# Hybrid decoder step, expert stage: bound-checked gather and scatter of taken slots, with expert outputs kept at a row of token and choice

## What is computed

```python
g_sel = argmax(t @ rc_w + rc_b)                  # one of 4 groups for each token
vals, idx = top_k(softmax(lf[g_sel]), 2)         # two of the 8 experts in it
eid = g_sel * 8 + idx                            # 32 experts in all
for e in range(32):
    h = silu(t @ w_gate[e]) * (t @ w_up[e])      # 1024 -> 512
    out = out + gates[:, e:e+1] * (h @ w_down[e])  # 512 -> 1024
```

## Time and profile before

| | |
|---|---|
| median of three runs | 1232.8 us |
| profiled execution, its own time | 1232.51 us |
| its span in the trace | 1230.7 us |
| TensorE busy | 1017.0 us (83%) |
| VectorE, ScalarE, GpSimd busy | 32%, 23%, 24% |
| bytes moved | 291.19 MB, mean 237 GB/s |

### The profile page before, as it was taken

How to read it: one execution, slowest core, us unless ns; L and a number is a source line. 1 busy time by engine, 2 the same in 40 slices (tenths; PEclk the granted TensorE clock), 3 DMA queues, 4 the chain that set the end, 5 groups by cost and what they waited for, 6 DMA issues and landing times.

```text
span 1230.7 us, 16173 instructions
## 1 busy us (share of the span) xinstructions
PE 1017.0 (83%) x6140; PEld 692.2 (56%) x6141; DVE 399.5 (32%) x678; ACT 281.5 (23%) x554; POOL 299.4 (24%) x480
## 2 busy tenths in 40 slices
PE   5999999896999974699964999999976778976760
PEld 3888789675674763577743555555533434543430
DVE  3998374532423328651233101011000001000006
ACT  3125224530222604341121121121201111111102
POOL 1000788884014593035002001010100000000003
PEclk8999999897997896899985999999999999999895
DMA  5685341110057550415464999999999999999976
GB/s 214 241 137 84 75 106 36 37 52 16 29 121 160 188 154 18 161 70 205 171 255 167 384 389 383 389 394 386 394 401 398 400 405 395 385 389 402 390 271 214
DMA packets 83814, 291.19 MB, mean 237 GB/s; under 512 B 33460, under 2 KB 35380, under 8 KB 74940
## 3 DMA queue, kind: packets, MB, share of 16 engines
q1 hardware_dynamic: 69304, 252.97, 57.1%
q0 software_dynamic: 6944, 23.83, 6.3%
q10 hardware_dynamic: 7524, 13.83, 3.1%
HBM read 260.75 MB, written 27.59 MB: 234 GB/s over the span
## 4 chain that ended last, share of the span: by engine, by line
PE 48%; DMA 16%; POOL 15%; DVE 8%; issue 7%; SPq 3%; ACT 1%; DVEq 0%; ACTq 0%; POOLq 0%
DMA sb_arena<-w_up 11%; PE ps L860 9%; PE ps L618 8%; PE ps L957 7%; PE ps L950 7%; PE ps L971 6%; DMA sb_arena<-w_gate 4%; SPq L470 3%; POOL sb_rec L525 2%; POOL sb_rec L526 2%; POOL sb_arena L529 2%; POOL sb_arena L528 2%; POOL sb_rec L527 2%; PE ps L932 2%; PE ps L730 1%
## 5 line engine op out<-in xcount | busy, mean ns | idle before, releaser
L618 PE MATMUL ps<-sb_arena 128*128 128x264 f32 (+1 forms) x1152 | 272.9, 399 | 6.1 <-DVE sb_arena L1330 6.1
L618 PEld LDWEIGHTS ps<-sb_arena 128*128 128x128 f32 x1152 | 224.4, 196 | 55.4 <-issue 12.3
L950 PE MATMUL ps<-sb_arena 128*64 128x256 f32 x1152 | 138.4, 395 | 35.2 <-DMA sb_arena<-w_gate 28.3
L1708 DVE TENSOR_TENSOR sb_sst<-sb_sst,ps 128x256 f32<-128x256 f32 x36 | 15.2, 421 | 450.7 <-PE ps L957 414.0
L971 PE MATMUL ps<-sb_arena 128*64 128x512 f32 x576 | 131.5, 598 | 26.8 <-DVE sb_arena L1713 26.8
L957 PE MATMUL ps<-sb_arena 128*64 128x256 f32 x1152 | 132.9, 384 | 20.9 <-DMA sb_arena<-w_up 20.9
L950 PEld LDWEIGHTS ps<-sb_arena 128*64 128x64 f32 x1152 | 86.3, 143 | 98.4 <-DMA sb_arena<-w_gate 39.5
L957 PEld LDWEIGHTS ps<-sb_arena 128*64 128x64 f32 x1152 | 83.2, 138 | 66.6 <-DMA sb_arena<-w_up 27.1
L581 POOL COPY sb_idc<-sb_idx 64x1 int32 x36 | 6.4, 178 | 439.2 <-ACT sb_arena L1271 439.1
L971 PEld LDWEIGHTS ps<-sb_arena 128*64 128x64 f32 x576 | 38.1, 136 | 97.1 <-issue 61.7
L1274 ACT ACTIVATE sb_kxf<-ps 128x512 f32<-128x512 f32 x36 | 21.5, 597 | 310.5 <-PE ps L971 310.5
(11 more groups left out here) (270 smaller groups left out, 1205.4 us busy)
## 6 DMA issues: line engine op xcount, KB each, us to landing
sb_arena<-w_gate SPq DMA_DIRECT2D x32, 2048.0 KB, 35.0
sb_arena<-w_up SPq DMA_DIRECT2D x32, 2048.0 KB
sb_arena<-w_down SPq DMA_DIRECT2D x32, 2048.0 KB
sb_arena<-wi SPq DMA_DIRECT2D x28, 512.0 KB, 4.1
ye_scr<-sb_kxf ACTq DMA_DIRECT2D x72, 128.0 KB
sb_arena<-w_out SPq DMA_DIRECT2D x4, 2048.0 KB, 8.3
ye_scr<-sb_arena SPq DMA_DIRECT2D x2, 2048.0 KB, 11.9
sb_arena<-wglu SPq DMA_DIRECT2D x8, 512.0 KB, 4.9
```

Of the source, the lines that this page charges most:

```text
L618: last = mm(ps[:, b0 + h, 0:t1 - t0], ring[w % 3][:, k, :], src[:, k, t0:t1], start=k == 0, stop=k == KD - 1)
L950: last = mm(ps[64 * r:64 * r + 64, 0, 0:256], xt[:, k, :], Wg[s][:, k, 256 * r:256 * r + 256], start=k == 0, stop=k == KD - 1)
```

## The change

Expert outputs no longer lie at a row of tile and slot, but at row 2 x token + choice of a `ye_scr` of 1,072 rows.

- The routing builds `row_of` (that row, for each slot) and from it `tok_of` (the token). A free slot has row 4096 and token 2048, beyond the last valid ones.
- The gathers get a bounds check, by which indices beyond the last token are passed over.
- POOL's loop also stores the outputs: after the gather for tile q + 4 it waits until ACT has moved the result of tile q, copies the tile's column of `row_of`, issues one bound-checked scatter of 64 rows of 4 KB, and waits until it has landed (`yst`) before it goes on. `yo` has two buffers in place of four; ACT waits for `yo_free` (the scatter of tile q - 2 has landed) before it overwrites one.
- ACT moves the result with two instructions of 64 partitions x 512, so that a row of 1,024 lies in one partition, and issues no DMA.
- The ten gathers at the end become five plain loads of 1 MB (the last of 24 rows of 8 KB) on SP's queue, each with both choices, after POOL's `ye_ready`.
- The zeroing and the waits for it go. The one-hot arrays move to other addresses, so VectorE waits for the stores of `x2` before it writes `oh_tile`.

```diff
-        ye_scr = scratch("ye_scr", [(MAXT + RING) * T, D])
+        ye_scr = scratch("ye_scr", [2 * N, D])
-        yo = [kxf[:, D + 512 * u:D + 512 * u + 512] for u in range(RING)]
+        yo = [kxf[0:T, D + 1024 * u:D + 1024 * u + 1024] for u in range(2)]
@@ sync @@
-            sp.wait_ge(u_zero, 1)
-            for i in range((MAXT - E) * T // P // 4):
-                sp.dma_start(ye_scr[...], U[:, 0:4 * D]).then_inc(ye_zero, 16)
-            sp.wait_ge(ye_zero, 32)
+            sp.wait_ge(u_zero, 1)
             sp.dma_start(gfin, a["gfin"].partition_broadcast(P)).then_inc(moe_ld, 16)
+            sp.wait_ge(ye_ready, 1)
+            for i, (t0, n) in enumerate(TT):
+                sp.dma_start(G[i][0:n], ye_scr[2 * t0:2 * (t0 + n), :].rearrange("(p k) d -> p k d", k=2)).then_inc(gy[i], 16)
@@ gpsimd, in the loop @@
                     nc.gpsimd.indirect_dma_start(xg[u], None, x2_scr, bass.IndirectOffsetOnAxis(ap=idc[u], axis=0),
+                                                 bounds_check=N - 1, oob_is_err=False).then_inc(gath[u], 16)
+                    pl.wait_ge(yev, it * RING + u + 2)
+                    nc.gpsimd.tensor_copy(rwc[u % 2], row_of[:, bass.ds(it * RING + u, 1)]).then_inc(rwc_done, 1)
+                    pl.wait_ge(rwc_done, it * RING + u + 1)
+                    nc.gpsimd.indirect_dma_start(ye_scr, bass.IndirectOffsetOnAxis(ap=rwc[u % 2], axis=0), yo[u % 2], None,
+                                                 bounds_check=2 * N - 1, oob_is_err=False).then_inc(yst, 16)
+                    pl.wait_ge(yst, (it * RING + u) * 16 + 16)
+                    pl.sem_inc(yo_free, 1)
-            for u in range(RING):
-                pl.wait_ge(yst[u], ((nt + RING - 1) // RING) * 32 + 32)
-            for i, (t0, n) in enumerate(TT):
-                for k in range(2):
-                    nc.gpsimd.indirect_dma_start(G[2 * i + k][0:n], None, ye_scr[0:MAXT * T, :], ...)
+            pl.sem_inc(ye_ready, 1)
@@ scalar, in the loop @@
-                    ac.wait_ge(yst[u], it * 32 + 32)
-                    act_(yo[u], ps[:, 4, :], ACT.Copy).then_inc(yev, 1)
-                    ac.wait_ge(yev, q + 2)
-                    for r in range(2):
-                        ac.dma_start(ye_scr[bass.ds(q * T, T), r * 512:r * 512 + 512],
-                                     yo[u][64 * r:64 * r + 64, :]).then_inc(yst[u], 16)
+                    ac.wait_ge(yo_free, q + 1)
+                    act_(yo[u % 2][:, 0:512], ps[0:64, 4, :], ACT.Copy)
+                    act_(yo[u % 2][:, 512:1024], ps[64:128, 4, :], ACT.Copy).then_inc(yev, 1)
@@ vector, routing @@
+            for k in range(2):
+                ts(below[:, :, k], cst[:, C_TOK:C_TOK + 5], -2.0, ABSENT - k, ALU.mult, ALU.add)
+            tt(below, below, bc(cst[:, C_VAL:C_VAL + 5], 2, 2), ALU.mult)
             dv.wait_ge(rank_mm, 1)
-            V.tensor_copy(slot[:], slf).then_inc(slot_done, 1)
+            last.then_inc(slot_done, 1)
+            dv.wait_ge(slot_done, 1)
+            dv.wait_ge(x2_st, 80)
             tt(oh_tile, bc(flat(stf), 2, IDXC), bc(io64[:, 0:IDXC], 1, 10), ALU.is_equal)
-            V.tensor_tensor(oh4, oh4, bc(cst[:, C_TOK:C_TOK + 5], 2, 2 * IDXC), ALU.mult).then_inc(oh_done, 1)
+            V.tensor_tensor(oh_tile, oh_tile, bc(flat(below), 2, IDXC), ALU.mult).then_inc(oh_done, 1)
-            V.tensor_copy(idx[:], ps[0:T, 6, 0:IDXC]).then_inc(tab_ev, 1)
+            ts(rows, ps[0:T, 6, 0:IDXC], -1.0, ABSENT, ALU.mult, ALU.add)
+            link(V.tensor_copy(row_of[:], rows))
+            ts(rows, rows, 0.5, -0.25, ALU.mult, ALU.add)
+            ts(rows, rows, MAGIC, MAGIC, ALU.add, ALU.subtract)
+            V.tensor_copy(tok_of[:], rows).then_inc(tab_ev, 1)
@@ vector, end @@
-                dv.wait_ge(gy[i], 32)
+                dv.wait_ge(gy[i], 16)
```

More of the change, by code:

```diff
@@ L74 @@
 MAGIC = 12582912.0
+ABSENT = 4096.0
 TWO_PI_HI, TWO_PI_MID = 6.28125, 0.0019340515136718750
@@ L180, in build @@
         xg = [part(4288 + 1024 * i, D, p=(0, T)) for i in range(RING)]
-        oh_row, oh_tile = part(4288, 10, T), part(4928, 10, IDXC)
+        oh_row, oh_tile = part(19568, 10, T), part(18544, 10, IDXC)
         xst = part(8384, D, p=(0, T))
@@ L200, in build @@
         t32, O1, O2, rank, cn = small(5, E), small(5, E), small(5, E), small(5, E), small(3, E)
-        slf, stf = small(5, 2), small(5, 2)
+        slf, stf, below = small(5, 2), small(5, 2), small(5, 2)
         Ob = small(5 * E // 2).bitcast(BF16).rearrange("p (i e) -> p i e", e=E)
@@ L204, in build @@
         assert rt[0] <= 22640
-        G = [part(10352 + 1024 * i, D) for i in range(10)]
+        G = [part(10352 + 2048 * i, 2, D) for i in range(5)]
         gfin = part(20592, D)
@@ L235, in build @@
         ssum = sb("ssum", [P, 5])
-        idx = sb("idx", [T, IDXC], I32)
+        tok_of = sb("tok_of", [T, IDXC], I32)
+        row_of = sb("row_of", [T, IDXC], I32)
         idc = [sb(f"idc{i}", [T, 1], I32)[:] for i in range(RING)]
+        rwc = [sb(f"rwc{i}", [T, 1], I32)[:] for i in range(2)]
         cum = sb("cum", [1, E + 1], I32)
-        slot = sb("slot", [P, 5, 2], I32)
         gate = sb("gate", [P, 2, 5])
@@ L304, in build @@
             "idc_done", "staged", "xtr", "xev", "gmm", "umm", "silu", "hr", "htr", "hev", "dmm", "yev"))
-        yst = [sem(f"yst{i}") for i in range(RING)]
+        rwc_done, yst, yo_free, ye_ready = sem("rwc_done"), sem("yst"), sem("yo_free"), sem("ye_ready")
         gy = [sem(f"gy{i}") for i in range(5)]
-        fin_done, fo_done, ye_zero = sem("fin_done"), sem("fo_done"), sem("ye_zero")
+        fin_done, fo_done = sem("fin_done"), sem("fo_done")
         gsrc = a["w_gate"].rearrange("e (p k) n -> e p k n", k=KD)
@@ L1255, in _ @@
             ac.wait_ge(slot_done, 1)
-            ac.wait_ge(ye_zero, 32)
             nt = tile_bound(ac, slice(E, E + 1), E)
-            for s_, v_ in ((silu, 1), (yev, 1), *((y, 32) for y in yst)):
+            for s_, v_ in ((silu, 1), (yev, 1), (yo_free, 2)):
                 ac.sem_inc(s_, v_)
@@ L1283, in _ @@
                 ac.wait_ge(fin_done, i + 1)
-                act_(G[2 * i][0:n], x1[i][0:n], ACT.Square, accum_out=ssum[0:n, i:i + 1]).then_inc(xs_sq, 1)
+                act_(G[i][0:n, 0], x1[i][0:n], ACT.Square, accum_out=ssum[0:n, i:i + 1]).then_inc(xs_sq, 1)
                 ac.wait_ge(root_in, 9 + i)
```

29 lines of the change are left out of this document (14 added, 15 removed).

## The result

The changed kernel takes **1205.11 us** (median of 4 runs, 1204.75 to 1205.86) against 1233.36 us for the kernel before (4 runs in the same comparison): a ratio of 0.9748, interval 0.9723 to 0.9772. The forecast was 1231.0 us. The rival called even relief, 1206.6 us, came within 1.5 us of it. The profiled execution has a span of 1203.6 us and took 1205.47.

A forecast was written before the change was run, and what follows sets the result against it. PE was taken to pace about the first 17 tiles, the weight stream the last 19. Routing +0.8, stream -3.2 and tail +0.9 gave -1.5 us from 1232.5 us: 1231.0 us, range 1224 to 1237 us.

The forecast's parts named there:

- even relief: Rival, late tiles: dropped rows relieve all DMA engines alike, saving 24.4 us plus 3.2 for four gathers; 1206.6 us, chance 0.26.
- the stream's part: Weight stream: four gathers beyond tile 36 go, -3.2 us; rows dropped from other gathers and stores gain 0.
- first rival: The rival even relief: a gain proportional to the dropped rows, 1206.6 us, chance 0.26.
- Its sign: What would show even relief: gates 15.5 to 16 us apart and the first wait for weights later than 880 us.
- The split of the 1.95 us: Tile traffic per one-tile expert in the weight stream: 1.14 us for two stores, 0.81 us for the gather.
- the four gathers beyond tile 36: Gathers after the last tile, wholly dropped while weights still load: 4 x 0.81 = -3.2 us.
- blocks of four: Four neighbouring rows dealt to each engine, so dropped rows rest only some engines and the pace stays: gain 0.
- Routing: Chain before the first gathers: four more linked operations +0.88 us, one cast less -0.08; +0.8 us, shifting the weight stream equally.
- POOL's round: POOL's loop: scatter landing plus 3.70 us, 12.9 us a tile, cost 0; rival that it binds, 1263 us, chance 0.10.
- The tail: From the last down product to the end: last moves, scatter landing 3.9 us, plain load 5.5 us; +0.9 us.
- Zeroing: Two stores of 2 MiB and their wait go; PE runs in one piece beside them, so 0.
- ACT: In the loop the move's second half adds 0.60 us a tile, two issues of 1.13 us go; slack, so 0.

The follow-up runs named there:

- the worst order of slots: Changed kernel with a tile's slots placed at rows 0 to 3, 16 to 19, 32 to 35, 48 to 51, then 4 to 7 and so on: 1220.57 us.
- the orders of slots: Changed kernel with a tile's slots at other partitions, 4, 8 or 16 rows apart or in fours: 1209.19, 1214.79, 1219.97 and 1220.57 us.
- 16 apart: Changed kernel with slot s of a tile at row 16 (s mod 4) + s div 4: 1219.97 us.

## Why the prediction was wrong

*The step that failed* is the choice in the stream's part, "Between a gain of 0 and a proportional one (first rival) I take 0", since "a share of an array is a run of neighbours". The two durations of the gather instruction on POOL said nothing of how rows reach the engines. The runs showed in its place that the stream is relieved by the rows dropped: its part came to -27.3 us in the loop where -3.2 stood, and moving all rows again cost 1237.41 - 1205.11 = 32.3 us. Even the worst order of slots kept 27.3 - 11.8 = 15.5 us of the loop's gain.

*The rival that came true was right in its mechanism and close in its sum*, 27.6 us against 27.3 measured over the loop; that it fits so closely is partly luck. Its early tiles, paced by PE and counted as 0, were worth 5 us when their rows were put back. Its sign, gates 15.5 to 16 us apart, holds for neither stretch alone (16.26 and 15.39), only for their mean, (97.56 + 76.95) / 11 = 15.86. And of the last 19 tiles not all wait for weights, as the forecast had it: from about 1036 to 1074 us gates come 12.70 us apart before and after, which is PE's pace. The DMA share beside them is 0.99 or more, so the stream still sets the end.

*The split of the 1.95 us was mis-sized*, at 0.81 us for a gather and 1.14 for two stores. By the runs a gather of 64 free rows costs 64 x 0.027 = 1.7 us (1.4 by the 0.022) and a scatter 64 x 4.0 / 801 = 0.3: nearly the same sum, the other way round. No run tells what the old stores of 2 KB rows took from the stream. The 0.57 of a window gave what they occupy, which need not be that, and the rest, 0.81, fell short of a gather's price. An estimate from the price of a free row: the four gathers beyond tile 36 were worth 4 x 1.7 = 6.8 us, not 3.2.

*The page that spoke for blocks of four* (the Trainium skill, "DMA: Bandwidth & Descriptors", section The descriptor swizzle) describes a transfer of 128 partitions; the orders of slots show that these 64-row transfers do not go by it. The 358 GB/s from HBM of the same page of the Trainium skill (section Specifications) are passed again, at 408.

*Routing was right on DVE, but not in what it does to the stream.* One cast became five operations, and the first gather's copy on POOL came 0.9 us later after the table's product. On DVE:

```profile
649.00 0.19 DVE L1309 TENSOR_SCALAR sb_arena<-ps 128x32 f32<-128x32 f32 x1 [0.24 <-PE ps L924]
...
659.69 0.21 DVE L1309 TENSOR_SCALAR sb_arena<-ps 64x56 f32<-64x56 f32 x1 [1.63 <-PE ps L930]
659.94 0.18 DVE L1706 CAST sb_row_of<-sb_arena 64x56 int32<-64x56 f32 x1
660.15 0.40 DVE L1309 TENSOR_SCALAR sb_arena<-sb_arena 64x56 f32<-64x56 f32 x2
660.59 0.18 DVE L1709 CAST sb_tok_of<-sb_arena 64x56 int32<-64x56 f32 x1
```

From the first operation to the last is 0.90 us (forecast 0.88). DVE still waits 0.24 us for the rank product, so the operations for `below` fitted in. Of the +1.3 us at the first gate, 0.6 stood there already at the rank product (649.00 us here, 648.39 in the earlier trace rows). But the load of `Wd[2]`, which waits for the fourth gather, is issued 3.4 us later and not 0.8, since by POOL's timeline the first of the four gathers ahead of the loop starts 2.0 us later and the others follow 2.0 us apart in place of 1.4. SP's queue before and then after:

```profile
668.14 0.37 SPq L464 DMA_DIRECT2D sb_arena<-w_down  x1
```

```profile
671.51 0.37 SPq L462 DMA_DIRECT2D sb_arena<-w_down  x1
```

No loss from it shows: the queue catches up and runs dry at 760 us.

*POOL's round does not bind, as forecast.* In the waits of the changed kernel (engine and line, releaser: us in total, times, longest) POOL waits for ACT in 34 of 36 tiles, and ACT's move (L1279) for PE in all 36 and for no buffer:

```profile
ACT sb_kxf L1279 <- PE ps L977: 314.9, 36, 12.1
POOL sb_idc L582 <- DMA ye_scr<-sb_kxf,sb_rwc: 249.8, 35, 9.2
POOL sb_rwc L590 <- ACT sb_kxf L1280: 111.6, 34, 14.0
```

The scatter's landing has a median of 7.9 us and 9.8 at most; the forecast took the gather's 9.2 in the median.

*The tail* was forecast at +0.9 us and came to -1.1:

```profile
1168.48 0.59 ACT L1279 ACTIVATE sb_kxf<-ps 64x512 f32<-64x512 f32 x1 [9.34 <-PE ps L977]
...
1170.90 0.93 POOL L593 DMA_INDIRECT ye_scr<-sb_kxf,sb_rwc  x1 [0.84 <-POOL sb_rwc L590]
1173.97 2.76 SPq L486 DMA_DIRECT2D sb_arena<-ye_scr  x5
...
1178.96 1.28 DVE L1312 SCALAR_TENSOR_TENSOR sb_arena<-sb_arena,sb_gate 128x1024 f32<-128x1024 f32 x1 [14.23 <-DMA sb_arena<-ye_scr]
```

From ACT's first move to the first sum is 10.48 us (11.30 in the earlier trace rows). The last scatter landed in 2.5 us, where 3.9 was taken from a gather, and the load lands after 4.9 us, where 5.5 was worked out: the two terms that no row showed.

*Zeroing* at 0 held (1203.25 us with it put back), and so did *ACT* at 0: its moves wait for PE.

## What to carry to other kernels

In a stage bound by DMA, price a transfer by what the stream beside it loses, by taking it away or adding it once, not by its bytes or the share it occupies. Small loads onto part of the partitions beside a full-width weight stream were two to four times as dear as their bytes here (0.022 to 0.041 us for 4 KB against 0.010), while scatters of the same rows cost half of theirs (4.0 us for 801 rows). A row that a bound check passes over leaves a packet of 0.01 us. Where PE sets the pace, little is gained by dropping rows: 5 of the 32.3 us here.

## What the runs showed that was not expected

- A load of 256 KB beside the stream cost 52 us over 36 tiles on 64 partitions and 89 us on 16; its source, and whether rows repeat, made no difference.
- Gathers slow the weight packets beside them (417 GB/s without, 385 with all rows); scatters do not (407 with the taken rows, 408 with all).
- A passed-over row remains as a packet of 4 bytes, 0.009 us on one engine in the median.
- Slots in plain order cost least; 16 apart cost 10.6 us in the loop at the same number of rows.
